# Gathered dot products instead of dense columns for 32 more tokens of a product-key expert layer

## The reference, cut to what matters

```python
def peer_block(h, w_q, sub_keys, u, v):
    ...
    experts = jnp.take_along_axis(cidx, top_p, axis=-1)     # 8 heads x 16 experts for each token, of 16384
    gate = jax.nn.softmax(top_s, axis=-1)
    act = jax.nn.gelu(jnp.einsum('nd,nhkd->nhk', h, u[experts]).astype(jnp.float32), approximate=False)
    return jnp.einsum('nhk,nhkd->nd', (gate * act).astype(h.dtype), v[experts])
```

## Time and profile before

| what | us |
|---|---|
| median of 3 runs | 4173.84 |
| the profiled execution | 4166.78 |
| its span in the profile | 4165.0 |
| U stage in it | about 1746 to 3006 |
| PE busy | 4079.6 (98%) |
| DVE busy | 2825.6 (68%) |
| POOL busy | 1378.9 (33%) |
| ACT busy | 1107.2 (27%) |

### The profile page before, as it was taken

How to read it: one execution, slowest core, us unless ns; L and a number is a source line. 1 busy time by engine, 2 the same in 40 slices (tenths; PEclk the granted TensorE clock), 3 DMA queues, 4 the chain that set the end, 5 groups by cost and what they waited for, 6 DMA issues and landing times.

```text
span 4165.0 us, 61697 instructions
## 1 busy us (share of the span) xinstructions
PE 4079.6 (98%) x25425; PEld 3651.8 (88%) x25425; DVE 2825.6 (68%) x3866; ACT 1107.2 (27%) x1398; POOL 1378.9 (33%) x1118
## 2 busy tenths in 40 slices
PE   8999999999999999999999999999999999999999
PEld 7999888988899999999999999999877777777777
DVE  4241465542434357698898888888678888888888
ACT  3112352222212121222232222222222222222223
POOL 1101000122000011036577788787034333334320
PEclk9999999999999999999999999999999999999999
DMA  7433227996465545356779999999889999999996
GB/s 199 124 106 101 90 66 197 267 284 209 146 213 195 183 98 115 71 131 132 191 181 276 292 296 294 296 295 294 253 307 350 361 352 356 354 360 347 361 336 236
DMA packets 587241, 969.76 MB, mean 233 GB/s; under 512 B 102849, under 2 KB 397761, under 8 KB 552520
## 3 DMA queue, kind: packets, MB, share of 16 engines
q1 hardware_dynamic: 345344, 415.28, 33.7%
q0 software_dynamic: 133040, 405.57, 30.4%
q10 hardware_dynamic: 108576, 144.97, 11.9%
HBM read 875.20 MB, written 85.95 MB: 231 GB/s over the span
## 4 chain that ended last, share of the span: by engine, by line
PE 89%; DMA 4%; DVE 4%; SPq 1%; issue 1%; ACT 1%; ACTq 0%; DVEq 0%
PE pair L2403 30%; PE pair L2053 27%; PE pair L2459 24%; DMA k_page<-in_cache_k_dram 3%; PE quad L2053 2%; PE quad L2447 1%; PE quad L2032 1%; DVE h_rows L1931 1%; PE pair L2091 1%; SPq L592 1%; DVE v_lo L1911 1%; PE quad L2376 0%; ACT w_hi L946 0%; PE quad L2139 0%; DVE kT_page L1571 0%
## 5 line engine op out<-in xcount | busy, mean ns | idle before, releaser
L2403 PE MATMUL pair<-act_hi,w_hi 128*128 128x448 f32 x2048 | 750.4, 366 | 3.3 <-DVE w_lo L1748 3.1
L2403 PE MATMUL pair<-act_lo,w_hi 128*128 128x448 f32 x2048 | 749.6, 366 | 0.0
L2403 PE MATMUL pair<-act_hi,w_lo 128*128 128x448 f32 x2048 | 749.6, 366 | 0.0
L840 POOL DMA_INDIRECT gmat_dram<-g_val,g_idx x384 | 648.4, 1689 | 264.5 <-DVE g_val L1823 118.6
L2053 PE MATMUL pair<-act_hi,w_hi 128*128 128x288 f32 x3264 | 716.8, 301 | 15.2 <-ACT tmp L1061 7.7
L2053 PE MATMUL pair<-act_hi,w_lo 128*128 128x288 f32 x3264 | 700.7, 296 | 0.0
L2053 PE MATMUL pair<-act_lo,w_hi 128*128 128x288 f32 x3264 | 699.7, 296 | 0.0
L1361 DVE TENSOR_TENSOR w_lo<-w_raw,w_hi 128x2048 fp32r<-128x2048 f32 x102 | 233.2, 2286 | 624.6 <-ACT w_hi L946 624.5
L2459 PE MATMUL pair<-v_hi,wx_hi 128*128 128x512 f32 x1512 | 598.2, 396 | 15.7 <-issue 9.0
L2459 PE MATMUL pair<-v_hi,wx_lo 128*128 128x512 f32 x1512 | 592.1, 392 | 0.0
L2459 PE MATMUL pair<-v_lo,wx_hi 128*128 128x512 f32 x1512 | 591.1, 391 | 0.0
(11 more groups left out here) (323 smaller groups left out, 5090.5 us busy)
## 6 DMA issues: line engine op xcount, KB each, us to landing
v_raw<-in_peer_v_dram SPq DMA_DIRECT2D x256, 512.0 KB, 7.4
w_raw<-in_peer_u_dram SPq DMA_DIRECT2D x262, 256.0 KB
w_raw<-in_peer_u_dram ACTq DMA_DIRECT2D x250, 256.0 KB
w_raw<-in_w_in_dram SPq DMA_DIRECT2D x44, 1024.0 KB
k_page<-in_cache_k_dram SPq DMA_DIRECT2D x256, 128.0 KB
gelu_dram<-tmp SPq DMA_DIRECT2D x128, 224.0 KB, 11.9
gmat_dram<-zeros SPq DMA_DIRECT2D x48, 512.0 KB, 7.2
a_back<-gelu_dram ACTq DMA_DIRECT2D x128, 192.0 KB, 7.4
```

The source lines that it names most:

```text
L840: pool.indirect_dma_start(out=gmat_cells, out_offset=bass.IndirectOffsetOnAxis(ap=g_idx[:, b, n:n + 1], axis=0), in_=g_val[:, b, n:n + 1], ...
L2403: op = m_(pair[0][:, n % 2, 0:TU], w[n % 2][:, k, :], x[:, k, 0:TU], start=(k == 0 and i == 0), stop=(k == KD - 1 and i == 2))
```

## The change

The 32 tokens 416 to 447 (the mid tokens) leave the dense product: TU becomes 416, and TS = 448 takes over its old meaning for the last 128 tokens. `gelu_dram` and the matmuls have 416 columns. The 32 tokens times 128 slots are laid out as four groups of 32 slots by 32 tokens on 128 partitions, so 32 more gathers and dots give their activations (`m_act`). Their row numbers (`m_slot`) come from the selection, their h is copied four times over the partitions by 4 groups of matmuls beside tiles 46 to 49 (`turn_mid`, `take_mid`) into `h_mid` in SBUF. N_DOT = 160 dots replace 128; they still have to be spread over tiles 27 to 123, 8 of them before tile 44. In the V stage 32 of the 64 gathers of activations go, and DVE transposes `m_act` into their place.

```diff
-TU = 448
-N_SU = T - TU
-N_CELL = TU - TV
-assert len(SUMS) == PK and SP_N * 4 == N_CELL
+TS, TU = 448, 416
+N_SU = T - TS
+N_CELL = TS - TV
+N_GATHER = TU - TV
+N_DOT = N_SU + PK * (TS - TU) // P
+TURN_MID = 46
+assert len(SUMS) == PK and SP_N * 4 == N_CELL and TS - TU == 32
...
-    return min(N_SU, DOTS_EARLY + (N_SU - DOTS_EARLY) * (n - SEL_END) // (DOT_TO - SEL_END))
+    return min(N_DOT, DOTS_EARLY + (N_DOT - DOTS_EARLY) * (n - SEL_END) // (DOT_TO - SEL_END))
...
             def gather_u(i):
+                rows = e_slot[:, i:i + 1] if i < N_SU else m_slot[:, i - N_SU:i - N_SU + 1]
                 pool.indirect_dma_start(out=u_rows[i % U_RING][:, :], out_offset=None, in_=u_rows_dram,
-                                        in_offset=bass.IndirectOffsetOnAxis(ap=e_slot[:, i:i + 1], axis=0)
+                                        in_offset=bass.IndirectOffsetOnAxis(ap=rows, axis=0)
                                         ).then_inc(u_row_in[i % U_RING], 16)
...
-                for t in batch_tokens(b):
+                for t in batch_tokens(b)[0:N_GATHER // SP_N]:
...
+            pool.wait_ge(top_done, N_PQ + 4)
             for b in range(2):
                 weigh(b)
...
+            def take_mid(r):
+
+                act.wait_ge(h_mm, H_MM + 4 + r + 1)
+                if r == 0:
+                    act.wait_ge(gates_ready, N_DENSE)
+                a.copy(h_mid[:, :].rearrange("t (q k r) -> t k q r", q=NQ, r=QR)[:, 4 * r:4 * r + 4],
+                       pair[1][:, r % 2, :].rearrange("t (k q r) -> t k q r", q=NQ, r=QR)).then_inc(h_ev, 1)
...
+                if 0 <= n - TURN_MID < 4:
+                    take_mid(n - TURN_MID)
...
+            act.wait_ge(dot_done, DOT + N_DOT)
             a.activation(s_act[:, :], s_act[:, :], ACT.Gelu).then_inc(a_gelu, 1)
+            a.activation(m_act[:, :], m_act[:, :], ACT.Gelu).then_inc(a_gelu, 1)
...
             def expert_slots(tb):
+                if tb == 3:
+                    mid = slice(TU - TV, TS - TV)
+                    for q in range(NQ):
+                        at = slice(q * QR, (q + 1) * QR)
+                        op = v.scalar_tensor_tensor(m_slot[quadrant(q), :], sel[mid, 0, at], float(P), sel[mid, 1, at], ALU.mult, ALU.add)
+                    link(op)
...
                 if i == 0:
                     dve.wait_ge(h_ev, 4)
+                if i == N_SU:
+                    dve.wait_ge(h_ev, 8)
+                h = quad[:, :, :].rearrange("p a c -> p (a c)") if i < N_SU else h_mid[:, :]
+                out = s_act[:, i:i + 1] if i < N_SU else m_act[:, i - N_SU:i - N_SU + 1]
                 dve.wait_ge(u_row_in[i % U_RING], 16 * (i // U_RING + 1))
-                v.tensor_tensor_reduce(out=u_rows[i % U_RING][:, :], in0=quad[:, :, :].rearrange("p a c -> p (a c)"),
+                v.tensor_tensor_reduce(out=u_rows[i % U_RING][:, :], in0=h,
                                        in1=u_rows[i % U_RING][:, :], scale=1.0, scalar=0.0, op0=ALU.mult, op1=ALU.add,
-                                       accum_out=s_act[:, i:i + 1]).then_inc(dot_done, 1)
+                                       accum_out=out).then_inc(dot_done, 1)
...
-                    dve.wait_ge(a_gelu, N_U + 1)
+                    dve.wait_ge(a_gelu, N_U + 2)
+                    v.transpose(e_act[:, N_GATHER:N_CELL], m_act[:, :]).then_inc(top_done, 1)
                     link(v.tensor_tensor(s_act[:, :], s_act[:, :], s_gate[:, :], ALU.mult))
...
+            def turn_mid(r):
+
+                pe.wait_ge(sel_tev, 3)
+                if r >= 2:
+                    pe.wait_ge(h_ev, 4 + r - 1)
+                for kk in range(4):
+                    for x in (act_hi, act_lo):
+                        for q in range(NQ):
+                            op = m_(pair[1][quadrant(q), r % 2, kk * P:(kk + 1) * P], x[:, 4 * r + kk, TU:TS].bitcast(F), ident[:, :],
+                                    start=(x is act_hi), stop=(x is act_lo), skip_group_check=True)
+                op.then_inc(h_mm, 1)
...
+                if 0 <= n - TURN_MID < 4:
+                    turn_mid(n - TURN_MID)
```

More of the change, by code:

```diff
@@ L205, in hybrid_step @@
         s_gate = r("s_gate", [P, PK])
+        m_slot = r("m_slot", [P, QR], U32)
+        m_act = r("m_act", [P, QR])
         r = Region(A_X, END)
@@ L285, in hybrid_step @@
         si_f = r("si_f", [P, 16, 16])
+        cand_at = r.at - BASE
         cand = r("cand", [P, PH, 256])
+        h_mid = Region(cand_at, END)("h_mid", [P, D])
         ts = r("ts", [P, PH, TOPK])
@@ L456, in hybrid_step @@
         E_IN = 16 * DB * PAGES // V_RING
-        S_IN = [16 * len(range(j, N_SU, U_RING)) for j in range(1, 1 + S_RING)]
-        s_done, S_DONE = x_scaled, 2 * TB + N_SU
+        S_IN = [16 * len(range(j, N_DOT, U_RING)) for j in range(1, 1 + S_RING)]
+        s_done, S_DONE = x_scaled, 2 * TB + N_DOT
         rows_read, ROWS_READ = pa_s, 4 * H
@@ L676, in load_v @@
                 sp.dma_start(v_raw[i % V_RAWS][:, :], v_tiles[:, n, half * D // 2:(half + 1) * D // 2]).then_inc(v_in[i % V_RAWS], 16)
-            sp.wait_ge(dot_done, DOT + N_SU)
+            sp.wait_ge(dot_done, DOT + N_DOT)
             for s in range(2):
@@ L682, in _ @@
             sp.dma_start(h_rows[0:NS, BLOCKS, :], h_dram[T - NS:T]).then_inc(rows_back, 16)
-            sp.dma_start(h_rows[NS:P, BLOCKS, :], h_dram[TU:T - NS]).then_inc(rows_back, 16)
+            sp.dma_start(h_rows[NS:P, BLOCKS, :], h_dram[TS:T - NS]).then_inc(rows_back, 16)
             sp.wait_ge(u_turn, 2 * N_U - 2)
@@ L705, in _ @@
             sp.dma_start(y_sample.rearrange("b t d -> (b t) d"), h_rows[0:NS, BLOCKS, :]).then_inc(y_out, 16)
-            sp.dma_start(y_prompt[0, TU:SEQ, :], h_rows[NS:P, BLOCKS, :]).then_inc(y_out, 16)
+            sp.dma_start(y_prompt[0, TS:SEQ, :], h_rows[NS:P, BLOCKS, :]).then_inc(y_out, 16)
             for tb in range(BLOCKS):
@@ L852, in _ @@
                 for i in dots_of(n):
-                    if i + U_RING < N_SU:
+                    if i + U_RING < N_DOT:
                         pool.wait_ge(dot_done, DOT + i + 1)
@@ L880, in weigh @@
             def weigh(b):
-                pool.wait_ge(back_in[b % 4], CELLS_IN[b % 4] + 16 * COLS * (b // 4 + 1))
+                pool.wait_ge(back_in[b % 4], CELLS_IN[b % 4] + 16 * (N_GATHER // SP_N) * (b // 4 + 1))
                 if b >= 2:
@@ L2434, in _ @@
                     turn_h(n)
+                if 0 <= n - TURN_MID < 4:
+                    turn_mid(n - TURN_MID)
             pe.wait_ge(a_gelu, N_U - 1)
             pe.wait_ge(sel_tev, 3)
-            pe.wait_ge(dot_done, DOT + N_SU)
+            pe.wait_ge(dot_done, DOT + N_DOT)
             def expert_sums(q):
```

## The result

The changed kernel took 4218.3 us in the median of 4 runs (4212.8 to 4234.6), beside 4171.8 for the kernel before: a ratio of 1.012, 95% interval 1.010 to 1.014. It is 1.2% slower, clear of the spread. The profiled execution took 4215.0 us (span 4213.2), 48.2 more in span than before.

What follows compares the result with a forecast made beforehand. PE and DMA were both taken as full in the U stage, the change relieving PE by loading DMA. From the profiled execution, 4166.8 - 20 + 75 + 4 - 2.6 = 4223 us; 8-in-10 range 4172 to 4288.

Steps and rivals of the forecast that it cites:

- PE's saving: Dense product of U: 189.3 ns a matmul, 9.09 us a tile instead of 9.73, 82 us over 128 tiles.
- copies of h: Tiles 46 to 49: 256 matmuls on PE take 10 to 16 us, partly covered by idle time; 4 us taken, bounds 0 and 16.
- Tiles 0 to 43: U stage, 1746 to 2180 us: DVE is the limit; 20 us saved, bounds 0 and 28.
- Tiles 44 to 123: U stage with the gathers: DMA ends last at 10.7 us a tile, 75 us more; bounds +63 and +115.
- 1.08 is full: Tiles 44 to 123: a DMA share of 1.08 without idle slices is the ceiling; 914 us of work takes 846.
- the +115 of the upper bound: Tiles 44 to 123: the extra 33.6 MB of gathers priced at the stretch's 292 GB/s.
- Last tiles: Tiles 124 to 127: no dots, PE's pace, 2.6 us saved.
- V stage: 32 gathers of cells less on POOL, the new wait and one more Gelu: taken as nothing.
- POOL, the second bound: Tiles 44 to 123: rival where DMA has room and POOL's 9.7 us a tile decides, 4148 us; chance 0.09.
- Latency of the ring: Tiles 44 to 123: rival where four gathers are latency-bound, 12.3 us a tile, 4354 us; chance 0.10, including PE clock loss.
- about 358 GB/s: Tiles 44 to 123: rival with the ceiling in bytes, DVE's 9.1 us a tile deciding, 4106 us; chance 0.05.
- most named signs: U stage some 55 us longer, middle tiles 10.5 to 11 us, PE and DVE waiting, DMA share 1.08 at 295 to 305 GB/s.

Runs made afterwards that it cites:

- two terms: The changed kernel with two of the three terms in the dense product of U, high by low left out: 4209.8 us, ratio 1.007.
- old width: The changed kernel with all its gathers, but PE multiplies 448 columns again, the last 32 unused: 4236.0 us, ratio 1.018.

## Why the prediction was right

The forecast was 4223 us, slower, for the reason that the experiments bear out. That it came within 5 us of the median is in part luck: the forecast rise was 56.4 us and the measured one 46.5, and the sum started from the profiled execution, 5 us below the median of the kernel before. Step by step:

- **PE's saving**: 189.3 ns a matmul forecast, 188.4 measured, 82 us in all. It is real: the run without extra gathers is 62 us faster than before, with the copies of h and DVE's early limit taking the rest.
- **Tiles 0 to 43**: 20 us saved forecast, 17.0 measured. DVE is the limit there, as said; PE waited 13.8 us for `w_lo` in 1746 to 2180 us of the changed kernel.
- **Tiles 44 to 123**: +75 forecast, +4 for the copies of h; +64.4 measured. The place, the sign and the resource were right, the size 14.6 us too high. The mis-sized term is the work of all engines. What is there already was priced at what it took before, and that shrank: the two hardware queues took 49.5% of 700 us for 72 tiles, 4.81 us a tile, and after the change 42.5% for 67, 4.44 us:

```profile
q0 software_dynamic: 51300, 132.18, 65.1%
q1 hardware_dynamic: 28695, 49.01, 24.9%
q10 hardware_dynamic: 19143, 34.86, 17.6%
```

  That is 0.37 x 80 = 30 us of engine time. The time of a packet is elastic: on q1 it fell from 109 to 97 ns in the mean. A gather, worked out as in the prediction, took 3.12 us of all engines, 3.09 before, where 2.95 was forecast for the added ones; that works the other way. So the premise "1.08 is full" was wrong, as the run without extra gathers and the one with half of them at 448 columns show. The kernel before ran a few per cent below the ceiling, and the estimate came out near because the added bytes were far more than that room. In bytes the sum is shorter, 3.25 MB a tile at 309 GB/s is 10.5 us, but 309 was only known afterwards: at the 292 of before it is the +115 of the upper bound.
- **The copies of h**: 10 to 16 us of PE forecast if uncovered. In the run without extra gathers 64 of the 256 stand in 1.90 us, 7.6 us in all, 30 ns each, below the lower price of 40.
- **Last tiles** -2.6 forecast, -4.8 measured; **V stage** 0 and +1.2; the +4.3 us before the first Gelu no step had.
- **Rivals.** POOL, the second bound, was priced right (9.7 us) and reached only with half the bytes. Latency of the ring did not show with 3 or 5 buffers. The Trainium skill (DMA: Bandwidth & Descriptors, section Bandwidth) gives about 358 GB/s as one core's limit from HBM, its share when both cores of a pair stream. This case doesn't show such a limit: over the last stage the rate was 337 GB/s after and 340 before, but single slices of 25 us there reach 392 and 395. Its U stage stayed at 318 or below in the mean whatever was tried.
- **What would show it**: most named signs came. But the U stage is 43 us longer, not 55; DVE's waits for raw tiles fell, from 73.9 to 18.5 us, in place of rising; the rate of 309 GB/s is above the 295 to 305 that I named; and ACT's waits for stores were not foreseen.
- **The range**: the bounds of the terms add up to 4199 and 4295, where the prediction wrote 4188 and 4290 for its likeliest case. The measured time lies within both.

## What to carry to other kernels

When work moves from a full engine to DMA, add up the bytes of a tile and divide by the rate that the stage reaches; 33.6 MB of gathers cost 112 us here, where the narrower product gave 62. A DMA share of 1 with no idle slice says that work is always queued, not that no more fits: only a run that asks for more, or for less elsewhere, finds the ceiling. The engine to relieve is the one whose removal shortens the time: a third of PE's matmuls could go here for 8.5 us.

## What the hardware showed unexpectedly

- At one DMA share, 1.07 to 1.08, the rate was 292 (before), 301 (two terms), 307 (no extra gathers), 309 (the change) and 315 GB/s (old width): the share is no gauge of the load once it is past 1. Each is one execution, and that of the old width was the fastest of its four.
- Fewer gathers in flight can be faster: 4242, 4191, 4218 and 4199 us with rings of 2, 3, 4 and 5. The order is not one of depth, and no run says why.
- An indirect DMA of 128 cells of 4 bytes costs POOL some 1.9 us with the gap before it. For DMA it is cheap: 96 of 384 less gave 13 us, and the runs of the two kernels overlap.
- PE's pauses of about a microsecond a tile left the granted clock at 0.98; with 28% of the time idle it was 0.82.
